# Modulation sums as rows in output groups, and q, k, v between the opening's modulation units

## The reference

```python
# first block, twice (l = 0, 1)
ada = c_act @ w_ada[l] + b_ada[l]                    # 1024 -> 3 * 1024
shift, scale, gate = jnp.split(ada, 3, axis=-1)
h = rmsnorm(x, norm_g[l]) * (1.0 + scale) + shift
p = h @ w_in[l]                                      # q, k, v, o, z of an mLSTM; q, k, v, z of a retention
...
x = x + gate * (y @ w_out[l])
# second block, twice: six vectors a layer (1024 -> 6 * 1024), a mixer (convolution and band attention),
# then a dense SwiGLU (l = 0) or a mixture of eight experts, two for each token (l = 1)
```

## Time and profile before

| what | us |
|---|---|
| median of three runs | 2087.67 (2086.46 to 2089.18) |
| the profiled execution, its own time | 2089.77 |
| its span, from the first to the last instruction | 2087.9 |
| TensorE matmuls busy | 2047.5 |
| VectorE busy | 1752.3 |
| ScalarE busy | 1322.0 |

### The profile page before, as it was taken

How to read it: one execution, slowest core, us unless ns; L and a number is a source line. 1 busy time by engine, 2 the same in 40 slices (tenths; PEclk the granted TensorE clock), 3 DMA queues, 4 the chain that set the end, 5 groups by cost and what they waited for, 6 DMA issues and landing times.

```text
span 2087.9 us, 33390 instructions
## 1 busy us (share of the span) xinstructions
PE 2047.5 (98%) x13347; PEld 1829.9 (88%) x13347; DVE 1752.3 (84%) x2155; ACT 1322.0 (63%) x1267; POOL 31.1 (1%) x60
## 2 busy tenths in 40 slices
PE   7999999999999999999999999999999999999998
PEld 5999999999999799999878888888888888888887
DVE  3898976888759778888768889898898989899897
ACT  3655555665645663435667777776777777777774
POOL 3000000000000000000000000000000000000000
PEclk8999999999999999999999999999999999999999
DMA  9787865766656569987548999999999999999995
GB/s 295 254 265 230 250 210 173 226 214 195 219 179 218 170 213 311 313 325 230 165 165 297 365 356 355 376 365 349 359 357 377 360 351 362 368 368 355 358 357 189
DMA packets 358817, 597.37 MB, mean 286 GB/s; under 512 B 10985, under 2 KB 204025, under 8 KB 358665
## 3 DMA queue, kind: packets, MB, share of 16 engines
q1 hardware_dynamic: 355248, 588.72, 82.0%
q0 software_dynamic: 2752, 5.86, 1.1%
q10 hardware_dynamic: 664, 0.66, 0.1%
HBM read 591.80 MB, written 4.22 MB: 285 GB/s over the span
## 4 chain that ended last, share of the span: by engine, by line
PE 78%; DVE 12%; ACT 3%; DMA 3%; issue 3%; SPq 1%; POOL 0%; DVEq 0%; POOLq 0%; ACTq 0%
PE ps L1729 10%; PE ps L1731 10%; PE ps L1730 10%; PE ps L1760 5%; PE ps L1759 5%; PE ps L1758 5%; PE ps L1203 3%; PE ps L1260 3%; PE ps L1204 3%; PE ps L1205 3%; PE ps L1261 3%; PE ps L1262 3%; DVE wlo L1827 3%; DVE acc L1883 3%; ACT whi L774 2%
## 5 line engine op out<-in xcount | busy, mean ns | idle before, releaser
L1827 DVE TENSOR_TENSOR wlo<-raw,whi 128x2048 fp32r<-128x2048 f32 x485 | 1108.7, 2289 | 190.2 <-ACT whi L774 187.6
L774 ACT CAST whi<-raw 128x2048 fp32r<-128x2048 f32 x485 | 926.4, 1911 | 350.4 <-PE ps L1731 123.3
L1203 PE MATMUL ps<-hhi,whi 128*128 128x256 f32 x1360 | 387.9, 285 | 0.0
L1204 PE MATMUL ps<-hlo,whi 128*128 128x256 f32 x1360 | 380.4, 280 | 0.0
L1205 PE MATMUL ps<-hhi,wlo 128*128 128x256 f32 x1360 | 380.2, 280 | 0.0
L1729 PE MATMUL ps<-whi,xghi 128*128 128x512 f32 x896 | 355.2, 396 | 0.7 <-DVE wlo L1827 0.7
L1731 PE MATMUL ps<-wlo,xghi 128*128 128x512 f32 x896 | 349.8, 390 | 0.0
L1730 PE MATMUL ps<-whi,xglo 128*128 128x512 f32 x896 | 349.1, 390 | 0.0
L1203 PEld LDWEIGHTS ps<-hhi,whi 128*128 128x128 f32 x1360 | 256.5, 189 | 3.9 <-issue 3.6
L1204 PEld LDWEIGHTS ps<-hlo,whi 128*128 128x128 f32 x1360 | 256.5, 189 | 0.2
L1205 PEld LDWEIGHTS ps<-hhi,wlo 128*128 128x128 f32 x1360 | 256.4, 189 | 0.0
(11 more groups left out here) (415 smaller groups left out, 2990.2 us busy)
## 6 DMA issues: line engine op xcount, KB each, us to landing
raw<-in_moe_w_gate_dram SPq DMA_DIRECT2D x112, 1024.0 KB, 6.0
raw<-in_moe_w_up_dram SPq DMA_DIRECT2D x112, 1024.0 KB, 6.2
raw<-in_moe_w_down_dram SPq DMA_DIRECT2D x112, 1024.0 KB, 5.2
raw<-in_w_in_dram SPq DMA_DIRECT2D x92, 1024.0 KB, 5.6
raw<-in_w_ada_dram SPq DMA_DIRECT2D x69, 1024.0 KB, 7.9
raw<-in_w_out_dram SPq DMA_DIRECT2D x24, 1024.0 KB, 5.2
raw<-in_ffn_w_gate_dram SPq DMA_DIRECT2D x11, 1024.0 KB, 8.8
raw<-in_ffn_w_up_dram SPq DMA_DIRECT2D x11, 1024.0 KB, 8.7
```

The lines of the kernel that those rows point to most:

```text
L774: nc.scalar.copy(whi[:, u.hl, :], raw[:, u.raw, :]).then_inc(hi_ready, 1)
L1203: mm(ps2[u.bank][:, j], whi[:, u.hl, w], hhi[:, k], start=k == 0, stop=False)
L1204: mm(ps2[u.bank][:, j], whi[:, u.hl, w], hlo[:, k], start=False, stop=False)
L1827: V.tensor_tensor(wlo[:, u.hl, :], raw[:, u.raw, :], whi[:, u.hl, :].bitcast(F32), ALU.subtract).then_inc(raw_free, 1)
```

## The change

1. A modulation unit beside heads and feed-forward is summed over the partitions into a row: a one-hot stationary operand of 32 columns puts the 256 sums into row `i // 4` of output group `i % 4`. `ada_sums` does this for three units one behind the other, in three different groups, at the places in `SUMMED_BEHIND` and `SUMMED_BEHIND_FF`. It waits for all three first.
2. The rows stay in one bank until the stage's end. ScalarE copies the bank once (`take_mod_row`), two matmuls turn it (`turn_mod`), and VectorE adds the bias in two pieces (`take_mods`), once a stage.
3. Six buffers hold VectorE's sums, three of them in `h`.
4. Layer 0 holds 12 units and layer 1 18, at new steps; the feed-forward units take one each behind fewer steps at its end.
5. In the opening, q's unit is issued behind the second modulation unit, k's and v's behind the fourth. Their products are made in pieces of two tiles between the sums of modulation units (`opening_products`), with three filling matmuls at one place. v goes to a bank of its own. The small loads of `c` and the identity move to ScalarE's queue.
6. In head 0 of layer 0, VectorE convolves q before k, o and z start with their high halves (`low_last_products`), and retention's q is multiplied before the values.

```diff
-ADA_START, ADA_TURN, ADA_MIX, ADA_FF = 8, (9, 6), (6, 4), 24
+ADA_START, ADA_HEADS, ADA_MIX, ADA_FF = 8, (12, 18), (6, 4), 24
+SLOTS = 6
-ADA_BESIDE = (((5, 7, 8, 9, 10, 13, 14, 15, 16), (1, 4, 5, 7, 8, 10, 13, 14, 16)),
-              ((4, 7, 9, 10, 13, 16), (1, 4, 7, 10, 13, 16)))
-ADA_SUMMED = (((7, 9, 10, 11, 12, 15, 16, 17, 17), (4, 6, 7, 8, 10, 11, 15, 16, 17)),
-              ((6, 9, 11, 12, 15, 17), (4, 6, 8, 12, 15, 17)))
+ADA_BESIDE = ((5, 8, 10, 13, 14, 16, 19, 22, 25, 28, 31, 34),
+              (5, 7, 8, 9, 10, 13, 14, 15, 16, 19, 22, 23, 25, 26, 28, 31, 32, 34))
+SUMMED_BEHIND = ({12: (0, 1, 2), 17: (3, 4, 5), 26: (6, 7, 8), 35: (9, 10, 11)},
+                 {10: (0, 1, 2), 15: (3, 4, 5), 17: (6, 7, 8), 25: (9, 10, 11), 29: (12, 13, 14), 35: (15, 16, 17)})
+SUMMED_BEHIND_FF = {4: (0, 1, 2), 8: (3, 4, 5), 12: (6, 7, 8), 16: (9, 10, 11), 20: (12, 13, 14),
+                    24: (15, 16, 17), 27: (18, 19, 20), 30: (21, 22, 23)}
+FF_BESIDE = [j for j in range(FF_UNITS) if j % 4 != 3] + list(range(FF_UNITS, FF_UNITS + 7))
...
-FIRST_UNIT_AT = 4
+UNITS_BEHIND, FIRST_UNITS, FIRST_V_BANK = {1: (0,), 3: (1, 2)}, 3, 4
...
+            def ada_sums(units):
+
+                for a, *_ in units[-1:] + units[:-1]:
+                    pe.wait_ge(ada_free, a.sums())
+                for a, *_ in units:
+                    n = ADA_FF if a.n >= A_FF else ADA_HEADS[a.n >= A_L1]
+                    g, r = GROUP * (a.i % 4), a.i // 4
+                    mm(ps[7][g:g + GROUP, 0:S], one_hot[:, GROUP - 1 - r:2 * GROUP - 1 - r], slots[a.n % SLOTS],
+                       start=a.i < 4, stop=a.i >= n - 4, skip_group_check=True).then_inc(ada_done, 1)
+
+            def turn_mod(times, n):
+
+                pe.wait_ge(arow_ready, times)
+                rows = -(-n // 4)
                 for j in range(2):
-                    last = mm(bank[:, a.col + j:a.col + j + 1], acc[:, a.n % HALF, j * P:(j + 1) * P], ones[:, 0:1],
+                    last = mm(ps[7][:, S + 4 * rows * j:S + 4 * rows * j + 4 * rows].rearrange("p (m g) -> p m g", g=4),
+                              mod_row[:, P * j:P * j + P], ident.rearrange("p (g m) -> p m g", g=4)[:, 0:rows],
                               start=True, stop=True)
-                last.then_inc(ada_done, 1)
-
+                last.then_inc(arow_turned, 1)
...
-            for a in ADA_AT_START:
-                n = a[0].n
-                ada_start(a[0])
-                if n == 1:
-                    norm(0)
-                if n >= 2 and n % 2 == 0:
-                    turn_rows(n // 2 - 1)
+            starts = [a[0] for a in ADA_AT_START]
+            ada_start(starts[0])
+            ada_start(starts[1])
+            norm(0)
+            turn_rows(0)
+            ada_start(starts[2])
+            ada_start(starts[3])
+            opening_products(0, (0, 1))
+            turn_rows(1)
+            keep_busy(OPENING_WAIT, 7)
+            opening_products(0, (2, 3))
+            opening_products(1, (0, 1, 2, 3))
+            ada_start(starts[4])
+            ada_start(starts[5])
+            opening_products(2, (0, 1))
+            turn_rows(2)
+            opening_products(2, (2, 3))
+            ada_start(starts[6])
+            opening_products(0, (4, 5))
+            ada_start(starts[7])
+            opening_products(1, (4, 5))
             turn_rows(3)
+            opening_products(2, (4, 5))
+            opening_products(0, (6, 7))
+            opening_products(1, (6, 7))
...
+                    high(Unit(S_B1))
+                    norm_pair(0, 0)
+                    take_rows(1)
+                    high(Unit(S_B1 + 1))
+                    norm_pair(0, 1)
+                    high(Unit(S_B1 + 2))
+                    for p in (2, 3):
+                        take_rows(p)
                         norm_pair(0, p)
...
             dve.wait_ge(std_ready, 1)
+            low(Unit(S_B1))
             for p in range(4):
                 modulate(p)
-                for k in ((), (0, 1, 2, 3), (4, 5), (6, 7))[p]:
+                for k in (2 * p, 2 * p + 1):
                     norm_low(0, k)
                 if p == 1:
-                    low(Unit(S_B1))
-            low(Unit(S_B1 + 1))
+                    low(Unit(S_B1 + 1))
+                    low(Unit(S_B1 + 2))
```

More of the change, by code:

```diff
@@ L802, in norm_std, with take_mod_row @@
                     .then_inc(std_ready, 1)
+            def take_mod_row(units):
+                act.wait_ge(ada_done, units)
+                nc.scalar.copy(mod_row, ps[7][:, 0:S]).then_inc(arow_ready, 1)
             def norm_pair(n, i):
@@ new lines, in low_last_products @@
+            def low_last_products(u, between=None):
+                pe.wait_ge(hi_ready, u.count())
+                for j in range(2):
+                    for k in range(KD):
+                        w, o = slice(256 * k + P * j, 256 * k + P * j + P), ps2[u.bank][:, j]
+                        mm(o, whi[:, u.hl, w], hhi[:, k], start=k == j == 0, stop=False, skip_group_check=True)
+                        mm(o, whi[:, u.hl, w], hlo[:, k], start=False, stop=False, skip_group_check=True)
+                if between:
+                    between()
+                pe.wait_ge(raw_free, u.free())
+                for j in range(2):
+                    for k in range(KD):
+                        w, o = slice(256 * k + P * j, 256 * k + P * j + P), ps2[u.bank][:, j]
+                        last = mm(o, wlo[:, u.hl, w], hhi[:, k], start=False, stop=k == KD - 1, skip_group_check=True)
@@ L2105, in _ @@
                                 else:
-                                    step.wait(back=3)
+                                    step.wait(back=2 * len(xs) - 1)
                                     last = V.scalar_tensor_tensor(qacc[:, x, t], src, w, qacc[:, x, t], ALU.mult, ALU.add)
@@ L2111, in _ @@
                                     step.mark(last)
+                    if hd.n == 0:
+                        gates_places(l)
+                        dve.wait_ge(taken_s, hd.count(7, 1))
+                        for tap in range(CONV_K):
+                            convolve(tap, (0,))
+                        gates_taken(l)
+                        low(k.plus(LOOK))
+                        dve.wait_ge(taken_s, hd.count(7, 2))
+                        for tap in range(CONV_K):
+                            convolve(tap, (1,))
+                        gates_summed(l)
+                        low(v.plus(LOOK))
+                    else:
+                        if h_no == 0:
+                            gates_places(l)
+                            gates_taken(l)
+                        dve.wait_ge(taken_s, hd.count(7, 2))
+                        for tap in range(CONV_K):
+                            if h_no == 0 and tap == 2:
+                                gates_summed(l)
+                            convolve(tap, (0, 1))
                     if h_no == 0:
```

267 lines of the change are left out of this document (142 added, 125 removed).

## The result

The changed kernel takes **2100.98 us**, median of 6 runs (2098.6 to 2103.4), against 2087.7 for the kernel before in runs on the same chip. The ratio is 1.0064, 95% interval [1.0053, 1.0074]: slower by 13 us, where 16 us less were forecast.

A forecast was written before the change was run, and what follows sets the result against it. TensorE, busy 98%, was taken as the bound wherever VectorE keeps up. Sums as rows -11.2, layer 0's fewer units -3.0, layer 1's more +1.5 and the opening -3.5 gave -16.2 us: 2071.5 us, range 2062 to 2081.

The forecast's parts named there:

- The sums as rows: All stages: 18 groups of three units at 0.65 us each replace 54 single sums, net -11.2 us.
- the rival with serial groups: Groups don't run side by side, so three units take six rounds: 14.8 us back, 2086.3 us; chance 0.05.
- -5.1 for the feed-forward part: Feed-forward part: TensorE's saving from sums as rows, -10.8 + 5.2 + 0.45 us.
- -1.1 for layer 1: Layer 1, 12 units become 18: TensorE's net from sums as rows, -5.4 + 3.9 + 0.45 us.
- -3.0 in layer 0, by six units fewer: Layer 0: with 12 units a late sum's 1.1 us wait and 1.9 us of lower clock go; 0 to -3.5.
- -5.0: Layer 0, 18 units become 12: TensorE's net from sums as rows, -8.1 + 2.6 + 0.45 us.
- +1.5 in layer 1 (0 to +5): Layer 1: six more units fit VectorE's free time barely; the same late sum at one chance in two.
- the half chance: Layer 1: one chance in two of a late sum for the unit beside step 16, summed behind 17; +1.5 us.
- -3.5 for the opening: Opening: v ends at 61.1 instead of 63.5 us, and o and z save 1.1 us; bounds -9 to +1.
- o and z no longer wait for the gate chain: Head 0 behind v: TensorE starts o's and z's high halves first, another 1.1 us saved.
- groups wait for their last unit: A late third unit holds TensorE, 3.0 us each place; eight late ones give 2095.5 us; chance 0.08.
- the opening gives nothing and layer 1 pays: Clock returns late in the opening (+4.5 us), VectorE's load costs layer 1 about 3 us: 2079 us; chance 0.22.

The follow-up runs named there:

- e5_ff_queue: The changed kernel with SyncE's modulation loads of the feed-forward stage issued one weight unit later: 2086.61 us, ratio 0.9995.
- e12: The kernel before with only SyncE's modulation loads of the feed-forward stage issued one weight unit later: 2087.24 us, ratio 1.0001.
- e3: The changed kernel with the whole opening and the order of head 0 of the kernel before: 2092.17 us, ratio 1.0022.
- e13: e9 with the gates' 24 products taken before v's, not behind six of its eight tiles: 2076.63 us, ratio 0.9947.
- e9: e8 with only q's weights loaded among the modulation units, k's and v's behind the eighth; head 0 as changed: 2081.03 us, ratio 0.9966.
- e8: e6 with the opening and head 0 as changed: 2082.12 us, ratio 0.9975.
- e7: e6 with q's weights alone loaded behind the second modulation unit, its products between the modulation units: 2073.34 us, ratio 0.9931.
- e6: The changed kernel with 15 units in each layer, the older opening and head 0, and later feed-forward modulation loads: 2074.42 us, ratio 0.9939.
- e10: e8 with head 0 in its order before the change: 2082.36 us, ratio 0.9974.
- e14: e13 with the turn of the gates also ahead of o's products: 2080.98 us, ratio 0.9967.

## Why the prediction was wrong

The forecast was -16.2 us and the measurement +13.3. Of the distance of 29.5 us, 12.6 lie in the feed-forward part, 9.2 in layer 0 with the opening, 4.2 in layer 1 and 1.7 behind; the rest is that the profile of the kernel before lay 2.1 us above its median and that of the changed kernel 0.3.

- **The sums as rows** run side by side, at the upper bound of their price. A group was forecast at 0.65 us between 0.45 and 0.75. Timeline of TensorE, e5_ff_queue, one group between products:

```profile
908.18 0.28 PE L1295 MATMUL ps<-fhi,wlo 128*128 128x256 f32 x1
908.40 0.40 PE L1331 MATMUL ps<-h 128*32 128x256 f32 x1
908.40 0.41 PE L1331 MATMUL ps<-acc,h 128*32 128x256 f32 x2
908.64 0.38 PE L1331 MATMUL ps<-h 128*32 128x256 f32 x1
908.64 0.39 PE L1331 MATMUL ps<-acc,h 128*32 128x256 f32 x2
908.96 0.39 PE L1293 MATMUL ps<-fhi,whi 128*128 128x256 f32 x1
909.18 0.28 PE L1294 MATMUL ps<-flo,whi 128*128 128x256 f32 x1
```

  Two rounds of 0.24 us, 0.56 us from the first to the next instruction: three units run side by side, and the rival with serial groups is out. Counted from the product ahead to the second one behind, where two steps of 0.12 us would be 0.24, a group costs 1.00 - 0.24 = 0.76 us. The stage terms came out all the same: -5.1 for the feed-forward part measured -5.1 to -5.2 once the queue is free, -1.1 for layer 1 measured -1.5 with its mixer. There is some luck in the first: eight groups at 0.76 would leave -4.3, and the stage before had 1.8 us of waits for single sums, which the prediction did not count and which e5 does not have.
- **-5.1 in the feed-forward part** is the step that failed worst: it came out +7.5. The working costed what TensorE saves and VectorE's load over 200 us (174.76 of them), so it took the transfers to keep up at no cost, and did not look at SyncE's queue behind the new step list, which stands in the diff: nine steps with a unit in a row, each with a modulation load ahead of a weight load. It cost 12.6 us between forecast and result, by far the largest part; the trace has it as 7.7 us of waits for `wlo` and 5.1 of lower clock.
- **-3.0 in layer 0, by six units fewer** came near as a sum: with the older opening layer 0 ends 7.7 us earlier with 12 units against the kernel before, 5.7 against e12, where -5.0 and -3.0 stood. The split between the two was wrong: with 18 units the rows alone give 3.2 at most, since VectorE was the bound.
- **+1.5 in layer 1 (0 to +5)** was too small: +4.6 with the -1.1 in it, so 5.7 for the six units, above the bound. By the trace these are the waits of 2.2 and 1.5 us and the 1.7 us of the clock; in e3, where the clock did not fall, the six units cost 4.0. That 10.4 us fit into 10.9 us of free time "barely" was read as fitting; but VectorE's free time in a period isn't where its units stand. The unit beside step 16 was late, 1.5 us at the group behind step 17, as the half chance had it; the scores' mask, 2.2 us late, was in no term. That 15 and 15 costs nothing in layer 1 was there to be had, and neither table of the change used it.
- **-3.5 for the opening** was wrong in sign: +5.4 at the end of layer 0. The step that failed is the last: "o and z no longer wait for the gate chain", another 1.1 us. The end of v came out nearly as worked, 62.05 for 61.1 against 63.5, and q's first products at 29.22 for 28.3, with the clock back at 36 to 37 for 37.5. But the sum followed TensorE to v's end and no further, and that is not what the rest of head 0 waits for. The gates' products had moved behind most of v, VectorE's first step on them came at 60.84 for 58.05, and TensorE then stood 6.5 us in head 0. e13 shows the place of these products for 4.4 us; for the rest the cause is open.
- **The rivals.** Of "groups wait for their last unit" one case of 18 appeared, 1.5 us in layer 1. It had each late group pay 1.9 us of clock too; the traces have the same waits both with a fall of the clock and without (the 2.2 us in the changed kernel and e3, the 2.7 us in e9 and e8), so that isn't so each time. In the kernel before three sums were late over the whole program (2.8 us), not one. Of "the opening gives nothing and layer 1 pays" the outcome came true and the reason for the opening did not, since the clock was back by 37 us. None held the mechanism with the largest loss. The chance of 0.07 for slower was far too small for a change whose new step tables were weighed by VectorE's average over a period or over 200 us.

What is left, 1.7 us behind the feed-forward part, is no effect of the change as far as is known: e5, with the same instructions there, has 0.2 us.

## What to carry to other kernels

When a step table changes, walk every queue through it, that of the engine that issues the transfers first: a load that waits for a buffer holds every load behind it, and a list with no free step can turn that into a loop that runs at the time from issue to landing. Loads issued one unit later gave nothing in the kernel before and 14 us in this one. An earlier end of the products is a gain only if the chain through the other engines starts no later: find the first instruction of that chain (here the gates' 24 products) and keep it ahead, before filling gaps. And price a wait of TensorE with what the clock may add: read the granted clock behind it before comparing two profiles.

The best version has sums as rows, 15 and 15 units, the later loads and q alone in the opening (e7): 2073.34 us, 0.9931 [0.9917, 0.9944] of the kernel before. Its distance from e6, which has the older opening, is 1.1 us and within the spread of both.

## What the runs showed of the hardware

- A weight load issued 0.4 us behind a modulation load took 7.17 to 8.56 us from issue to landing in the loop, while the engines of the transfers stood at a share of 0.80. At the 350 GB/s of the earlier trace rows its 1.05 MB would take 3.0 us and the two loads together 6.0 (an estimate). Four loads are issued in a turn of 15.23 us, and over the window at 920 us they moved 285 GB/s where e5_ff_queue moved 337: the waits between them made the turn, not the rate of the engines.
- Three matmuls of 32 columns in three different output groups take two rounds of 0.24 us, like those in four groups, with about 0.1 us over, and the first product behind them takes 0.22 us instead of 0.12. The Trainium skill, page TensorEngine Tiling (Array Packing), section Key Properties, has the engine drained at a change of mode; the trace agrees in so far as this is all it can cost here.
- Every stretch below full clock that was read from 60 to 980 us cost 1.7 us or twice that: in the changed kernel 1.7, 3.4 and 1.7 at 439, 906 and 940 us, in e9 1.7 at 78, in e10 3.4 at 66, in e14 1.7 at 100. The same wait was followed by one in some executions and not in others: 2.2 us in layer 1 in the changed kernel but not in e3, 2.7 us for `wlo` in e9 but not in e8.
- In the opening of the changed kernel the granted clock was 0.50 at 35 us and 0.87 in the window at 36; TensorE had worked without a gap since 29.22, with three filling matmuls at 33.28. Before, it rose only at 46, behind work without a gap since 39.49. The filling matmuls are not what brings it back each time: in e8, with the same opening, it was 0.74 in the window at 31 and full at 32, and they start at 31.97.
